# Two adaLN blocks computed behind the FFN in place of ahead of it, and the mLSTM output scaled by ScalarE in a hybrid diffusion step

## The reference

```python
mod = (jax.nn.silu(cond) @ w_ada + b_ada)            # per layer: shift, scale, gate (x2)
xp = xp + p_g1 * yp                                   # first half of a layer
xp = xp + p_g2 * fp                                   # second half
# layer 0, first half: Hyena long convolution beside a bidirectional mLSTM
h = num / max(abs(den), exp(-m_t))                    # each direction; the two are added
h = rmsnorm(h, ml_norm_g) * sigmoid(o)                # over each head of 128 columns
y = concat([y_hy, h]) @ w_out
```

## Time and profile before

| | |
|---|---|
| median of 3 runs | 1374.6 us (1373.92 to 1376.81) |
| the profiled execution | 1374.98 us, its span 1373.1 us |
| PE busy | 1321.2 us (96%) |
| DVE busy | 1045.9 us (76%) |
| ACT busy | 816.6 us (59%) |
| mean granted clock of TensorE | 0.990 |
| moved by transfers | 408.14 MB, mean 297 GB/s |

### The profile page before, as it was taken

One profiled execution on the slowest core, in us unless ns is written; L12 is line 12 of the kernel. 1 busy time (PEld: TensorE's weight loads), 2 busy tenths in 40 slices (PEclk: granted clock), 3 DMA queues, 4 the chain that ended last, 5 costly groups with the idle time before them and its releaser, 6 DMA issues.

```text
span 1373.1 us, 16270 instructions
## 1 busy us (share of the span) xinstructions
PE 1321.2 (96%) x6307; PEld 1032.8 (75%) x6307; DVE 1045.9 (76%) x1011; ACT 816.6 (59%) x920; POOL 75.6 (6%) x81
## 2 busy tenths in 40 slices
PE   5999988999999989999999999999999999999997
PEld 2676646788886777788888888888888888888875
DVE  0584787555446753788998898998988988988996
ACT  2444324533335374677767767776777777777663
POOL 1102100000002000000000000000000000000370
PEclk9999999999999989999999999999999999999998
DMA  9979997855556633599999999999999999999992
GB/s 349 347 254 313 325 335 254 284 187 184 184 184 198 216 130 125 182 318 365 365 352 351 346 347 366 366 347 338 345 356 362 365 357 331 348 363 366 342 351 92
DMA packets 289591, 408.14 MB, mean 297 GB/s; under 512 B 15342, under 2 KB 223497, under 8 KB 289445
## 3 DMA queue, kind: packets, MB, share of 16 engines
q1 hardware_dynamic: 282048, 391.23, 83.8%
q0 software_dynamic: 3904, 11.59, 2.8%
q10 hardware_dynamic: 3556, 4.21, 0.9%
HBM read 401.99 MB, written 1.87 MB: 294 GB/s over the span
## 4 chain that ended last, share of the span: by engine, by line
PE 84%; DVE 8%; DMA 4%; ACT 1%; issue 1%; SPq 0%; POOL 0%; DVEq 0%; ACTq 0%
PE bank L1908 81%; DVE w_lo L550 3%; DMA raw<-in_w_ada 2%; PE bank L2258 2%; DMA Gb<-arena 1%; DMA raw<-in_ev_w_in 1%; PE bank L1966 1%; ACT w_hi L543 0%; DMA Gb<-gate_rows 0%; SPq L657 0%; ACT arena L1169 0%; DVE sml L1723 0%; PE bank L2379 0%; PE bank L2416 0%; DVE arena L1649 0%
## 5 line engine op out<-in xcount | busy, mean ns | idle before, releaser
L550 DVE TENSOR_TENSOR w_lo<-raw,w_hi 128x2048 fp32r<-128x2048 f32 (+1 forms) x238 | 549.0, 2309 | 157.0 <-ACT w_hi L543 155.4
L543 ACT CAST w_hi<-raw 128x2048 fp32r<-128x2048 f32 (+1 forms) x238 | 451.5, 1898 | 121.7 <-PE bank L1908 82.7
L1908 PE MATMUL bank<-w_hi,x_hi 128*128 128x512 f32 x1072 | 431.1, 402 | 7.5 <-DVE x_lo L1336 2.3
L1908 PE MATMUL bank<-w_lo,x_hi 128*128 128x512 f32 x1072 | 420.4, 392 | 0.0
L1908 PE MATMUL bank<-w_hi,x_lo 128*128 128x512 f32 x1072 | 419.3, 391 | 0.0
L1908 PEld LDWEIGHTS bank<-w_hi,x_hi 128*128 128x128 f32 x1072 | 201.3, 188 | 53.2 <-issue 8.7
L1908 PEld LDWEIGHTS bank<-w_hi,x_lo 128*128 128x128 f32 x1072 | 201.5, 188 | 45.2
L1908 PEld LDWEIGHTS bank<-w_lo,x_hi 128*128 128x128 f32 x1072 | 201.7, 188 | 38.8 <-issue 0.2
L550 DVE TENSOR_TENSOR w_lo<-arena,w_hi 128x2048 fp32r<-128x2048 f32 x88 | 203.0, 2307 | 33.1 <-ACT w_hi L543 32.9
L543 ACT CAST w_hi<-arena 128x2048 fp32r<-128x2048 f32 x88 | 168.3, 1912 | 28.8 <-PE bank L1908 28.8
L1908 PE MATMUL bank<-w_hi,g_hi 128*128 128x512 f32 x440 | 175.0, 398 | 3.4 <-DVE g_lo L1607 3.4
(11 more groups left out here) (300 smaller groups left out, 963.5 us busy)
## 6 DMA issues: line engine op xcount, KB each, us to landing
raw<-in_moe_w SPq DMA_DIRECT2D x352, 512.0 KB, 5.5
arena<-in_moe_w SPq DMA_DIRECT2D x176, 512.0 KB, 5.6
raw<-in_w_ada SPq DMA_DIRECT2D x96, 512.0 KB, 6.6
raw<-in_ff_w SPq DMA_DIRECT2D x66, 512.0 KB, 4.5
raw<-in_ev_w_in SPq DMA_DIRECT2D x28, 512.0 KB, 7.7
raw<-in_at_w_qkv SPq DMA_DIRECT2D x12, 512.0 KB, 5.1
raw<-in_ev_w_out SPq DMA_DIRECT2D x8, 512.0 KB, 5.7
Gb<-gate_rows POOLq DMA_DIRECT2D x8, 512.0 KB, 5.0
```

The costliest lines, as they stand in the source:

```text
L543: nc.scalar.copy(w_hi[:, t % SPL, c], place[:, c]).then_inc(hi_ok, 1)
L550: nc.vector.tensor_tensor(w_lo[:, t % SPL, c], raw_slot(n)[0][:, c], w_hi[:, t % SPL, c].bitcast(F32), ALU.subtract).then_inc(lo_ok, 1)
L1908: return pe.matmul(out, lhsT, rhs, start=start, stop=stop)
```

## The change

- The list of tiles has the adaLN blocks in their own order. Phase 1 is blocks 4 to 15 and phase 2 blocks 16 to 23, so blocks 22 and 23 (halves 44 to 47) are computed behind the QKV projection's loads, and everything in phase 2 moves by two blocks: ahead of the FFN PE takes halves 32 to 35, behind it 36 to 42, behind QKV 43 to 47. Ten idle products behind the FFN and four behind QKV go.
- Four halves (39, 40, 42, 45) have places of their own in the arena (`APART`), outside the ring, and are loaded during the FFN. SP waits there for the use of FF[0] and for the stored states.
- ACT scales all six parts of the mLSTM output (four numerators, two carried parts), with the weight times the inverse denominator made beforehand by one small DVE product; DVE adds. ACT also squares and sums the heads and scales them; DVE multiplies by the gate per token group. The norm's gain is loaded to `stage`, early.
- PE makes fft(2) ahead of ada(14). Half 31 comes behind the last inverse transform. Of the first layer's gates 32 rows are stored at once, of the second layer's 32.
- `wait_inputs` takes the token group: a projection's first half tile starts when that group's own input part is there.
- ACT makes high(OUT[0]) ahead of `stage_rows(1)` and high(OUT[1]) behind `take_turned`.

The diff, cut:

```diff
-        mgain = ar(6144, 512)
+        mgain = stage[:]
...
-        ADA_BLOCKS = (*range(16), 22, 23, *range(16, 22))
+        stream, ada_half_of, IN, AD = [], [], [], {}
...
-        for i in range(13, 18):
+        for i in range(13, 16):
...
+        APART_AT = {9: 39, 14: 40, 19: 42, 24: 45}
         for j, kind_chunk in enumerate(order(NCH)):
             if j == 2:
-                put_ada(18)
-                put_ada(19)
+                put_ada(16)
+                put_ada(17)
+            if j in APART_AT:
+                put_ada_half(APART_AT[j])
             put(FF, kind_chunk)
         QKV_BLOCKS = (2, 0, 1)
         for j, t in enumerate([t for w in QKV_BLOCKS for t in halves(a["at_w_qkv"][0], 512 * w)]):
             put(QKV, t)
             if j == 0:
-                put_ada(20)
-                put_ada_half(42)
+                put_ada(18)
+                put_ada_half(38)
             if j == 1:
-                put_ada_half(43)
-        put_ada(22)
-        put_ada(23)
+                put_ada_half(41)
+        for i in (43, 44, 46, 47):
+            put_ada_half(i)
...
+        APART = {AD[h]: c for h, c in zip(APART_AT.values(), (0, 2048, 5632, 14080))}
+        ring = [n for n in range(MOE0) if n not in APART]
+        def raw_turn(n):
+            return n - sum(m < n for m in APART)
...
-        PHASES = ((0, 4), (4, 18), (18, 24))
+        PHASES = ((0, 4), (4, 16), (16, 24))
...
-                if n >= RAW:
-                    tile_free(sp, n - RAW)
+                if n in APART:
+                    sp.wait_ge(used, sp_of(FF[0]) + 1)
+                    sp.wait_ge(stored_st, STATE_STORES)
+                elif raw_turn(n) >= RAW:
+                    tile_free(sp, ring[raw_turn(n) - RAW])
...
+                if p == 1:
+                    eng.wait_ge(rows_ok, 3)
...
+            warm(ACT.Sqrt)
+
+            def scale_heads(dst, src, scales):
+                for h in range(NH):
+                    c = slice(P * h, P * h + P)
+                    ins = sc.activation(dst[:, c], src[:, c], ACT.Identity, scale=scales[:, h:h + 1])
+                return ins
+
+            def scale_part(ready, dst, b, scales):
+                eng.wait_ge(nu_ok, ready)
+                scale_heads(dst, bank[b], scales).then_inc(pt_a, 1)
+
+            def head_squares(g):
+                for h in range(NH):
+                    ins = sc.activation(hyT0[:, g, P * h:P * h + P], xn[:, g, HW + P * h:HW + P * h + P], ACT.Square,
+                                        accum_out=sml[:, 32 + 4 * g + h:33 + 4 * g + h])
+                ins.then_inc(hs_q, 1)
+
+            eng.wait_ge(rd_ok, 1)
+            scale_part(1, xn[:, 0, HW:2 * HW], 4, sml[:, 72:76])
+            scale_part(2, xn[:, 1, HW:2 * HW], 5, sml[:, 76:80])
+            eng.wait_ge(cv_ok, 5)
+            scale_part(2, hyT0[:, 0, :], 0, sml[:, 0:4])
+            scale_part(3, hyT0[:, 2, :], 4, sml[:, 80:84])
+            eng.wait_ge(cv_ok, 6)
+            scale_part(4, hyT0[:, 1, :], 5, sml[:, 84:88])
+            scale_part(4, hyT0[:, 3, :], 1, sml[:, 4:8])
+            eng.wait_ge(pa_d, 2)
+            head_squares(0)
+            eng.wait_ge(pa_d, 4)
+            head_squares(1)
+            eng.wait_ge(hs_q, 2)
+            sc.activation(sml[:, 40:48], sml[:, 32:40], ACT.Sqrt, bias=C("eps"), scale=1.0 / HD).then_inc(hs_r, 1)
+            eng.wait_ge(hs_i, 1)
+            for g in range(G):
+                scale_heads(xn[:, g, HW:2 * HW], xn[:, g, HW:2 * HW], sml[:, 48 + 4 * g:52 + 4 * g]).then_inc(hs_s, 1)
...
+            high(OUT[0])
             stage_rows(1)
-            eng.wait_ge(hs_q, 1)
-            sc.activation(sml[:, 40:48], sml[:, 32:40], ACT.Sqrt, bias=C("eps"), scale=1.0 / HD).then_inc(hs_r, 1)
-            high(OUT[0])
+            take_turned(1, None)
             high(OUT[1])
-            take_turned(1, None)
-            gate_rows_out()
+            gate_rows_out(0)
...
+            v_.tensor_tensor(tiny, rden[:, :, 4:8], w_in_, ALU.mult).then_inc(rd_ok, 1)
...
+            def add_part(g, part, at):
+                eng.wait_ge(pt_a, part)
+                hs = xn[:, g, HW:2 * HW]
+                v_.tensor_tensor(hs, hs, hyT0[:, at, :], ALU.add).then_inc(pa_d, 1)
 
             fft_product(1)
             short_conv(4)
             hyena_gate(1)
-            head_rows(0)
             short_conv(5)
-            head_rows(1)
             fft_product(2)
-            head_rows(2)
+            add_part(1, 3, 0)
+            add_part(0, 4, 2)
+            eng.wait_ge(pa_d, 1)
+            add_part(1, 5, 1)
+            hyena_gate(2)
+            eng.wait_ge(pa_d, 3)
+            add_part(1, 6, 3)
             eng.wait_ge(kr_ok, 1)
             for d in range(NDIR):
                 ins = v_.scalar_tensor_tensor(kw[:, d], heads(bank[0][:, :]), HD ** -0.5,
                                               bc(cols[:, 3, 32 * d:32 * d + 4], HD), ALU.mult, ALU.mult)
             ins.then_inc(kw_ok, 1)
-            hyena_gate(2)
-            head_rows(3)
-            link(v_.tensor_tensor(sq, hall, hall, ALU.mult))
-            v_.tensor_reduce(sml[:, 32:40], sq.rearrange("p g (h n) -> p (g h) n", h=NH), AX, ALU.add
-                             ).then_inc(hs_q, 1)
+            eng.wait_ge(hs_r, 1)
+            v_.reciprocal(sml[:, 48:56], sml[:, 40:48]).then_inc(hs_i, 1)
             fft_product(3)
             eng.wait_ge(ld_mg, 16)
             eng.wait_ge(tj_t, 15)
             link(v_.tensor_tensor(sigo, sigo, mgain.unsqueeze(1).to_broadcast([P, G, HW]), ALU.mult))
-            link(v_.tensor_tensor(hall, hall, sigo, ALU.mult))
-            eng.wait_ge(hs_r, 1)
-            link(v_.reciprocal(sml[:, 48:56], sml[:, 40:48]))
             for g in range(G):
-                hg = heads(xn[:, g, HW:2 * HW])
-                link(v_.tensor_tensor(hg, hg, bc(sml[:, 48 + 4 * g:52 + 4 * g], HD), ALU.mult))
+                hs = xn[:, g, HW:2 * HW]
+                eng.wait_ge(hs_s, g + 1)
+                ins = v_.tensor_tensor(hs, hs, sigo[:, g, :], ALU.mult)
+                if g == 0:
+                    eng.wait_ge(iz_ok, 3)
+                    ins.then_inc(rows_ok, 1)
+            link(ins)
             hyena_gate(3)
             eng.wait_ge(iz_ok, 4)
-            for g in range(G):
-                eng.sem_inc(rows_ok, 1)
+            eng.sem_inc(rows_ok, 1)
...
+            def wait_inputs(s, i, g=1):
+
+                need = 2 * i + g + 1 if s in MODULATED else 2 * g + i + 1
+                eng.wait_ge(x_l, inputs_split(s) - 4 + need)
...
+            fft(2)
             ada(14)
-            fft(2)
-            eng.wait_ge(nu_t, 1)
+            eng.wait_ge(pt_a, 1)
             for h in range(NH):
                 ins = mm(bank[4][:, P * h:P * h + P], ST[:, 8 + h, :], vrow[:, 0, P * h:P * h + P], True, True)
             ins.then_inc(nu_ok, 1)
-            eng.wait_ge(nu_t, 2)
-            for h in range(NH):
-                ins = pe.transpose(bank[0][:, P * h:P * h + P], kT[:, h, 0:T], ident)
-            ins.then_inc(kr_ok, 1)
-            ada(15)
-            inverse_fft(2)
             eng.wait_ge(ld_C[1], 16)
+            eng.wait_ge(pt_a, 2)
             for h in range(NH):
                 mm(bank[5][:, P * h:P * h + P], ST[:, 12 + h, :], vrow[:, 1, P * h:P * h + P], True, True)
                 ins = mm(bank[1][:, P * h:P * h + P], qT[:, h, T:2 * T], stateC[1][:, h, :], True, True)
             ins.then_inc(nu_ok, 1)
-            ada(16)
+            eng.wait_ge(pt_a, 3)
+            for h in range(NH):
+                ins = pe.transpose(bank[0][:, P * h:P * h + P], kT[:, h, 0:T], ident)
+            ins.then_inc(kr_ok, 1)
+            inverse_fft(2)
+            ada_half(30)
             fft(3)
             eng.wait_ge(kw_ok, 1)
-            eng.wait_ge(nu_t, 4)
+            eng.wait_ge(pt_a, 5)
             for d in range(NDIR):
                 for h in range(NH):
                     k_ = kw[:, d, h, :]
@@ -2202,12 +2241,13 @@
             for d in range(NDIR):
                 ins = mm(bank[0][32 * d:32 * d + 32, :], onz[:, 31:63], kw[:, d], True, True)
             ins.then_inc(cs_ok, 1)
-            ada(17)
             inverse_fft(3)
+            ada_half(31)
+            eng.wait_ge(cs_t, 2)
+            turn_half(1, 0)
+            turn_half(1, 1)
             eng.wait_ge(den_t, 1)
-            eng.wait_ge(cs_t, 3)
             ada_cols(1)
...
-            ada(20)
+            ada(18)
+            ada_half(38)
+            ada_half(39)
+            ada_half(40)
+            turn_rows(3)
+            ada_half(41)
             ada_half(42)
-            idle_products(0, 7)
-            turn_rows(3)
-            ada_half(43)
-            idle_products(0, 3)
...
-            ada(22)
-            idle_products(6, 7)
+            ada_half(43)
+            ada_half(44)
+            ada_half(45)
+            idle_products(6, 3)
```

(20 more changed lines are left out.)

132 lines of the change are left out of this document (49 added, 83 removed).

## The result

Eight runs of each kernel on one chip: before 1374.73 us (1371.33 to 1376.81), after **1366.53 us** (1363.79 to 1369.76). The ratio is 0.9939, 95% interval 0.9924 to 0.9954. The forecast was 1365.6, in a range of 1361.5 to 1371.0. So the time came out as forecast; several of its terms did not, and their errors nearly cancel.

A forecast was written before the change was run, and what follows sets the result against it. DVE was taken to bound the mixer's end (174 to 211 us), PE the FFN. Terms of 7.6 + 0.5 + 1.25 - 0.3 = 9.05 us less gave 1365.6 us from a median of 1374.6, range 1361.5 to 1371.

The forecast's parts named there:

- DVE's balance and order: Mixer's end: mLSTM work taken off DVE, order laid out anew; OUT starts at 203.45 for 210.79, 7.3 us less.
- the 1.8 us at the reciprocal: Mixer's end: DVE waits at the reciprocal for ACT's squares and roots, giving back 1.8 us.
- My own bound for this, 8.2 less: OUT's start with four scalings at 1.15 us and quicker squares: roots 0.9 us earlier, 8.2 less in all.
- The wait by token group: Projections wait for one group's input: 1.2 us at OUT (counted in its 7.3), 0.5 at QKV, 1.25 at attention's output.
- The moved blocks at nothing: Mixer: ada(16) and ada(17), 3.7 us of PE beside DVE work, leave; their going is costed at nothing.
- Gate store, 0.3 less: Between OUT and the FFN: one store of gate rows in place of two, 0.3 us less.
- mgain, 0.3: POOL's queue: mgain's early load delays the chain's wait for Gb<-arena; 0.3 us more, bounds 0 and 0.9.
- Behind the FFN: Adaln halves replace idle products, hidden; FF[9] asked for not before some 251; QKV 0.5, attention's output 1.25 us less.
- ACT's chain: Rival, chance 0.13: at the mixer's end ACT's chain takes the place of DVE's; 1369.3 us.
- The clock: Rival, 0.08: PE's 3.1 us pause before inverse_fft(3) drops the clock, 1370.6 us; better attention clock, 1362.6, has 0.10.
- The idle products: Rival, 0.05: without them the clock falls before QKV, which starts at 1.2 GHz; slower, half of QKV gives 1382.
- Doesn't reach the end: Rival, 0.07: the adaLN tile landing at 240.06 doesn't move; 6 of 7.6 us given back, 1371.6 and up.

The follow-up runs named there:

- e3_mlstm: Kernel before plus the mLSTM output split between ACT and DVE, with adaLN blocks and wait for inputs as before: 1369.39 us, ratio 0.9960.
- a2_after: The kernel after, unchanged, run once more in a later set: 1367.40 us, ratio 0.9939.
- e2_blocks: Kernel before with only the two adaLN blocks moved behind the FFN: 1374.81 us, ratio 0.9998.
- e4_squares: Kernel after with ACT's four squares of the second group made twice: 1368.84 us, ratio 0.9950.
- e5_stay: Kernel after without the two adaLN blocks' move and without ada(15)'s new places: 1365.94 us, ratio 0.9947.
- e6_oldwait: Kernel after with the old wait for all lows of the inputs: 1366.19 us, ratio 0.9950.

## Why the prediction was right

The main step was right: DVE's work was the bound, and taking it off brings most of the gain (e3_mlstm alone 5.5 us of 8.2). The forecast lies within 0.9 us of the result by luck in part: OUT came 1.9 us earlier than forecast, the way from there to the FFN was 1.45 worse than forecast, and later terms 0.7.

*DVE's balance and order.* Right in kind. OUT was forecast 7.3 us earlier and came 9.3 earlier (8.7 in a2_after). Counted from fft(2)'s start both profiles took 22.90 us, where 24.47 was laid out. The miss is in ACT's terms. Four scalings were taken at 1.5 and took 1.14: I chose the row with two pointers; the row with one, 1.15, was the right one. The Trainium skill's estimate (ScalarE: Activation LUTs, section What ACT_TABLE_LOAD costs), 1.26, is above the measured value too, yet nearer than mine. With the squares at 0.30 each, the 1.8 us at the reciprocal became 0.48. My own bound for this, 8.2 less, was short too: kw came 1.0 us before its laid-out time, and high(OUT[0]), laid out to end at 200, ended at 197.3 (start 195.44), so that low(OUT[0]) at 198.51 waited for nothing.

*The wait by token group.* Right: 1.15 us at OUT for 1.2; 2.1 in all alone, for 1.2 + 0.5 + 1.25 of which OUT's share can be hidden. The attention output's 1.25 was 0.85 in profiles whose clock held.

*The moved blocks at nothing.* **The step that failed.** It was read from the old profile, where DVE hid them, and for the time of the blocks alone (e2_blocks) it holds. The reading was loose even there: "PE waited for DVE behind both", but of the two the old trace has a wait only behind ada(17), 1.36 us; behind ada(16) fft(3) follows at once (193.57). In this change they leave together with DVE's work, and beside that the halves between the transforms cost 2.8 us at OUT: by my estimate 0.7 to 1.9 for the blocks and the rest for ada(15), which the change also places elsewhere. The sentence "cover gone, PE would have been short of it" had the mechanism; I then priced it with the cover in place. My layout of DVE's order used PE's times with the blocks gone and ada(15) at its new places (fft(3) done at 190.9), so the 2.8 stood in the sum without a name, and the time came out. Of the time at the end no run shows a part that is due to the blocks.

*Gate store, 0.3 less.* Right for its own piece (from OUT to the store 0.45 less), but from OUT to the FFN it took 1.2 us more (5.4 in a2_after), by slower landings of the store and the spread. The two lows behind the adds are no new term: they were there before. It takes most of the surplus at OUT: 8.1 at the FFN for 7.6 forecast.

*mgain, 0.3.* Too small: 2.0 (0.6 to 3.4). It did not work through the last DMA of the Hyena rounds, as I had it, but perhaps through the input projection's tiles.

*Behind the FFN.* Right: QKV's clock stayed at 1.00 without the idle products, and the tiles apart were asked for at 251.05, where "not before some 251" was forecast, with nothing behind them.

*The rivals.* ACT's chain is on the path (e4_squares) but with 0.48 of waiting, so it did not decide. The clock did not fall at the mixer's pause of 1.58, and does at 2.75 (e4_squares), at 4.22 (e2_blocks) and, ahead of OUT, at 2.50 (e3_mlstm); pauses of 2.33 and 2.31 in the kernel before left it at 1.00, so the length of one pause does not tell it alone. The idle products were not missed. "Doesn't reach the end" named the right tile and place; 1.2 was given back on the way there, not 6.

## What to carry to other kernels

Work that is hidden on one engine has no price of its own: when the engine that hides it is lightened in the same change, price it again in the new order. A run that puts one part of a change back must put back nothing else: e5_stay moved ada(15) with the blocks, and so cannot say what the blocks were worth. Behind a wait for a transfer, look at what is queued on that engine that doesn't need it, and put it ahead. A small load moved ahead of others in a queue can cost more than its bytes; its place deserves a run of its own, and here its old place gave 2 us, give or take 1.4.

## What the runs showed of the hardware

Two things were not expected. The same store of 16 KB took 3.41 and 4.15 us in two profiles of the kernel after, and the spread behind it 5.80 and 8.19 (5.07 before); in e6_oldwait the same store took 1.38. And the attention stage's granted clock falls at other places in each profile of one kernel (between 490 and 510 us in the first profile after, nowhere in the attention in a2_after): from QKV to the attention's output it took 91.6 and 88.3 us. The 10.5 us by which the attention's output started earlier in the first profile than before is so no gain of the change beyond 8.4 plus 0.85; a reading of one profile against another says little there below 3 us.
